# Feed-forward up projections as seven 2x2 block products (Strassen) instead of eight, on one Trainium2 core

## The reference, cut to what matters

```python
def _swiglu(h, w13, w2):            # w13: 1024 x 5632, w2: 2816 x 1024
    g, u = jnp.split(h @ w13, 2, axis=-1)
    return (jax.nn.silu(g) * u) @ w2

def _sublayer(x, fn, pre_g, post_g, shift, scale, gate, res_w):
    h = _rmsnorm(x, pre_g) * (1.0 + scale[:, None, :]) + shift[:, None, :]
    y = _rmsnorm(fn(h), post_g)
    return x + res_w * (1.0 + gate[:, None, :]) * y
```

## Time and profile before

| what | value |
|---|---|
| median of the runs | 3217.52 us |
| lowest to highest | 3217.0 to 3223.48 us |
| span of the profiled execution, first to last instruction | 3213.7 us |
| PE busy | 3045.3 us (95%) |
| PE weight loads busy | 2461.7 us (77%) |
| DVE busy | 1728.6 us (54%) |
| ACT busy | 1155.9 us (36%) |
| POOL busy | 1349.1 us (42%) |
| mean DMA rate | 114 GB/s |

### The profile page before, as it was taken

The page is one execution under the profiler, slowest core; times in us unless marked ns, Lnnn a source line. Parts: engine busy times, 40 slices in busy tenths (PEclk is TensorE's granted clock), DMA queues, the critical chain, the costliest instruction groups (busy, mean ns, idle before and its releaser), DMA issues. The chain is left out here.

```text
span 3213.7 us, 52487 instructions
## 1 busy us (share of the span) xinstructions
PE 3045.3 (95%) x20065; PEld 2461.7 (77%) x20065; DVE 1728.6 (54%) x3224; ACT 1155.9 (36%) x2075; POOL 1349.1 (42%) x893
## 2 busy tenths in 40 slices
PE   5999999899999999999999999999888889999998
PEld 4888876678887888877788887987666667778887
DVE  6445478654445566232666114537677754674443
ACT  3222235432223322234332223226544434435343
POOL 3444443244444434453434444224767660143332
PEclk8999999999999999999999999999999999999999
DMA  7655432155544554332255334213222233222222
GB/s 216 195 184 173 158 85 73 53 170 183 183 156 153 167 180 135 97 90 79 86 163 151 94 93 136 79 53 112 65 58 58 56 107 73 91 77 71 82 66 59
DMA packets 641381, 366.02 MB, mean 114 GB/s; under 512 B 107902, under 2 KB 634132, under 8 KB 640688
## 3 DMA queue, kind: packets, MB, share of 16 engines
q1 hardware_dynamic: 633216, 351.57, 37.2%
q10 hardware_dynamic: 6640, 10.49, 1.1%
q0 software_dynamic: 1344, 1.44, 0.2%
HBM read 334.27 MB, written 24.97 MB: 112 GB/s over the span
## 5 line engine op out<-in xcount | busy, mean ns | idle before, releaser
L270 POOL TENSOR_TENSOR w_lo<-w_raw,w_hi 128x1024 fp32r<-128x1024 f32 (+1 forms) x333 | 786.6, 2362 | 1316.6 <-ACT w_hi L262 1263.9
L335 PE MATMUL acc<-h,w_hi 128*128 128x512 f32 x2256 | 704.4, 393 | 0.0
L262 ACT ACTIVATE w_hi<-w_raw 128x1024 fp32r<-128x1024 f32 (+1 forms) x332 | 344.6, 1038 | 941.1 <-PE acc L335 687.9
L335 PEld LDWEIGHTS acc<-h,w_hi 128*128 128x128 f32 x2256 | 417.3, 188 | 84.6 <-issue 1.8
L335 PE MATMUL acc<-h,w_lo 128*128 128x512 f32 x1128 | 440.3, 390 | 0.0
L335 PE MATMUL acc<-hid,w_hi 128*128 128x512 f32 x1056 | 326.3, 390 | 0.0
L716 DVE SCALAR_TENSOR_TENSOR ada_part<-ada_raw,c_act,ada_part 128x256 f32<-128x256 f32 x672 | 315.0, 489 | 18.6
L335 PEld LDWEIGHTS acc<-h,w_lo 128*128 128x128 f32 x1128 | 211.7, 188 | 45.8
L335 PEld LDWEIGHTS acc<-hid,w_hi 128*128 128x128 f32 x1056 | 197.3, 188 | 40.7
L335 PE MATMUL spare<-h,w_hi 128*128 128x512 f32 x688 | 211.7, 389 | 0.0
L335 PE MATMUL acc<-hid,w_lo 128*128 128x512 f32 x528 | 205.6, 389 | 0.0
(11 more groups left out here) (700 smaller groups left out, 6094.7 us busy)
## 6 DMA issues: line engine op xcount, KB each, us to landing
w_raw<-in_ffn_w SPq DMA_DIRECT2D x240, 512.0 KB, 4.0
ada_raw<-in_ada_w SPq DMA_DIRECT2D x88, 1024.0 KB, 5.0
w_raw<-in_od_w_in SPq DMA_DIRECT2D x32, 512.0 KB, 4.0
w_raw<-in_ffn_w SPq DMA_DIRECT2D x32, 384.0 KB, 3.1
w_raw<-in_ev_w_in SPq DMA_DIRECT2D x22, 512.0 KB, 3.9
image<-inverse_wait SPq DMA_DIRECT2D x144, 64.0 KB, 2.1
first_ada<-in_ada_w SPq DMA_DIRECT2D x8, 1024.0 KB, 12.4
w_raw<-in_ab_w_in SPq DMA_DIRECT2D x16, 512.0 KB, 4.0
```

The source lines that it names most:

```text
L262: act.activation(K.w_hi[:, first % SPLIT, 0:tiles, :], K.raw[:, first % RAW, 0:tiles, :], ACT.Copy).then_inc(K.hi_ready, 1)
L270: pool.tensor_tensor(K.w_lo[:, first % SPLIT, 0:tiles, :], K.raw[:, first % RAW, 0:tiles, :], K.w_hi[:, first % SPLIT, 0:tiles, :].bitcast ...
L335: mm = pe.matmul(out, w[:, slot, k, :], moving(ap, k, tokens), start=first and k == 0 and p == 0, stop=last and k == tiles - 1 and p == le ...
```

## The change

The up products of turns 3 to 21 are made in another way (turns 0 to 2 stay, `PLAIN = 3`). Tokens are halved (`HALF` = 256) and so is the depth of the product (`KH` = 4 of 8 blocks). With g and u as the two rows, this is a 2x2 by 2x2 block product, and seven block products p = 1 to 7 replace eight. Each is 4 tiles x 3 passes = 12 products of 256 columns.

- The four sums of h blocks (`term`, 1024 elements each) are made once a sub-layer by DVE, with hi parts by ACT (`term_hi`) and lo parts by DVE (`term_lo`). For them h is needed in full: ACT writes every h block twice (L501, L503), and DVE's lo part is now `full - hi`, both in SBUF.
- The four sums of weights are made each turn by DVE (`sums_first`, `sums_second`: one op of 1024 elements, two of 512). ACT makes seven hi parts and POOL seven lo parts of 512 elements a turn, one turn ahead of TensorE, in two sets of slots.
- The products land in seven half banks of PSUM. ACT copies product 1 to SBUF; DVE combines them (`combine_left`, `combine_right`, `combine_outer`), ACT takes silu, DVE the gated product (`gated`). The next turn's product 1 waits for `left`, product 5 for `u_second`, product 3 for `outer`.
- The gated values are kept in full (`hid_full`) and split into hi and lo only after the last turn: hi by ACT (`hidden_hi`), lo by DVE for 17 of 22 and by POOL for values 8 to 12. The first down turn waits tile by tile.
- Modulation chunks: one vector of one chunk a turn, in three pieces (`ada_part`) between the combinations, by a table; sub-layer 0 has 19 in its up turns and 7 in its down turns, 2 has 19 and 8, 3 has 11 of one vector and 4 of two vectors (a vector a turn) and 8 of two in its down turns, 5 has 4 of two and 8 of two.
- Loops over turns are written out. The scratch of the DMA descriptors is made 8192 bytes.

```diff
-def quick_pre_act(act, K, S, base, shift, update=True, between=None):
+def quick_pre_act(act, K, S, base, shift, update=True, between=None, full=None):
...
         act.activation(S.h[:, HI, b, :], S.tp[b % 2][:], ACT.Identity, bias=shift[:, b:b + 1]).then_inc(S.h_hi, 1)
+        if full is not None:
+            act.activation(full[:, b, :], S.tp[b % 2][:], ACT.Identity, bias=shift[:, b:b + 1]).then_inc(S.h_full, 1)
...
     def low(b):
+        if full is not None:
+            dve.wait_ge(S.h_full, b + 1)
+            dve.tensor_tensor(S.h[:, LO, b, :], full[:, b, :], S.h[:, HI, b, :].bitcast(F32), ALU.subtract).then_inc(S.h_ready, 1)
+            return
...
+        def slots_free(eng, t):
+            if t >= PLAIN + 2:
+                eng.wait_ge(S.turn_done, t - PLAIN - 1)
...
+                for t in range(PLAIN + 2, FB):
+                    n = base + 2 * t
+                    sp.wait_ge(S.lo, 7 * (t - PLAIN - 1))
+                    chunk_load(n + 1, up.sources[1](t))
+                    sp.wait_ge(S.left_done, t - PLAIN - 1)
+                    chunk_load(n, up.sources[0](t))
+                    ada_until(t)
...
+                for t in turns:
+                    for p in (1, 5, 7, 2, 6, 3, 4):
+                        lo(t, p)
...
+                for j in range(8, 13):
+                    pool.wait_ge(S.hid_hi, j + 1)
+                    pool.tensor_tensor(hid[:, j, :], hid_full[:, j, :], hid_hi(j).bitcast(F32),
+                                       ALU.subtract).then_inc(S.hid_pool, 1)
...
+                def product(t, p):
+                    pe.wait_ge(S.lo, 7 * (t - PLAIN) + LO_PLACE[p])
+                    for k in range(KH):
+                        for part in (HI, LO):
+                            pe.matmul(out_of[p], hi_of(t, p)[:, k, :], moving[p][:, part, k, :], start=k == 0 and part == HI, stop=False)
+                    for k in range(KH):
+                        mm = pe.matmul(out_of[p], lo_of(t, p)[:, k, :], moving[p][:, HI, k, :], start=False, stop=k == KH - 1)
+                    if p in done:
+                        mm.then_inc(done[p], 1)
...
+                    if tau == 0:
+                        pe.wait_ge(S.prod_ready, 2)
+                        pe.wait_ge(S.h_full, DB)
+                        pe.wait_ge(S.t_ready, 4)
+                    else:
+                        pe.wait_ge(S.left, tau)
+                    product(t, 1)
+                    product(t, 2)
...
+                    product(t, 6)
+                    if tau:
+                        pe.wait_ge(S.u_second, tau)
+                    product(t, 5)
+                    product(t, 7)
+                    if tau:
+                        pe.wait_ge(S.outer, tau)
+                    product(t, 3)
+                    product(t, 4)
...
+                def sums_first(t):
+                    tau = t - PLAIN
+                    slots_free(dve, t)
+                    chunk_landed(dve, t, 0)
+                    chunk_landed(dve, t, 1)
...
+                    dve.tensor_tensor(both, quarters[:, 2:3].broadcast_to([P, 2, KH * P]), quarters[:, 0:4:3],
+                                      ALU.subtract).then_inc(S.sums, 1)
+                    dve.wait_ge(S.sums, 3 * tau + 1)
+                    dve.tensor_tensor(sum_full(t, 6), full_of(t, 1), sum_full(t, 5),
+                                      ALU.subtract).then_inc(S.sums, 1)
...
+                for t in turns:
...
+                    if t > PLAIN:
+                        combine_outer(t - 1)
+                    if t + 1 < FB:
+                        sums_first(t + 1)
+                    if t > PLAIN:
+                        gated(t - 1)
+                    ada_piece(0, 2)
+                    combine_left(t)
+                    if t + 1 < FB:
+                        sums_second(t + 1)
+                    ada_piece(2, 5)
+                    combine_right(t)
+                    if pending is not None:
+                        ada_write(dve, K, S, ada, pending)
+                    ada_piece(5, DB)
...
+                hidden_lo(0, 4)
+                combine_outer(FB - 1)
+                hidden_lo(4, 8)
+                gated(FB - 1)
+                hidden_lo(13, FB)
```

More of the change, by code:

```diff
@@ new lines, in ada_load, with ada_landed, ada_part @@
+def ada_load(sp, K, q):
+    source, i = K.ada_of(q)
+    if q >= ADA:
+        sp.wait_ge(K.ada_used, FIRST_ADA + q - 1)
+    sp.dma_start(K.ada_raw[:, q % ADA], source(i)).then_inc(K.ada_landed[q % ADA], 16)
+def ada_landed(dve, K, q):
+    dve.wait_ge(K.ada_landed[q % ADA], 16 * (q // ADA + 1))
+def ada_part(dve, K, S, steps, q, v, lo, hi):
+    source, i = K.ada_of(q)
+    final = v == source.vecs - 1
+    for k in range(lo, hi):
+        col = K.cact[:, source.use[v], k:k + 1]
+        out = K.ada_acc[:, v, :] if k == DB - 1 else S.ada_part[:, v, :]
+        if k == 0:
+            if v == 0:
+                ada_landed(dve, K, q)
+            ins = dve.tensor_scalar(out, K.ada_raw[:, q % ADA, k, :], col, None, ALU.mult)
+        else:
+            steps.all()
+            ins = dve.scalar_tensor_tensor(out, K.ada_raw[:, q % ADA, k, :], col, S.ada_part[:, v, :], ALU.mult, ALU.add)
+        if k == DB - 1 and final:
+            ins.then_inc(K.ada_used, 1)
+        else:
+            steps.start(ins)
@@ L909, in ffn_phase, with ada_write @@
+def ada_write(dve, K, S, steps, q):
+    source, i = K.ada_of(q)
+    ada_columns(dve, K, steps, FIRST_ADA + q, source.bias(i), source.out(i), source.vecs, S.ada_cols)
 def ffn_phase(K, index, layer, sub, which):
     nc, A = K.nc, K.A
-    seg = K.weights.phases[index]
-    up, down = seg[:-1], seg[-1]
-    u0 = up[0]
+    up, down = K.weights.phases[index]
+    base = up.base
     shift, scale, gate = (K.mod_cols(layer, sub, kind) for kind in range(3))
     tiles = (8, 8, FB - 16)
+    turns = range(PLAIN, FB)
+    count = len(turns)
@@ L950, in _ @@
+                for c in range(2, 3 * DB):
+                    split_lo(pool, K, down, c // 3, c // 3, c % 3, tiles[c % 3])
                 split_next(pool, K, index, split_lo)
@@ L1036, in _ @@
-                for n in range(4):
-                    block_turn(n, n)
-                loop(pe, 4, DB, 4, block_turn)
+                        multiply(pe, K, down, n, n, j, tiles[j], [(banks[n % 4][:], LAT)],
+                                 lambda p, k, sl, j=j: hid_hi(8 * j + k) if p == HI else hid[:, 8 * j + k, :],
+                                 first=j == 0, last=j == 2, before=(lambda k, j=j: operand_ready(8 * j + k)) if n == 0 else None)
+                    if n == 0 and pending is not None:
+                        ada_pe(pe, K, FIRST_ADA + pending, K.ada_of(pending)[0].vecs, K.ada_acc, S.ada_cols)
```

430 lines of the change are left out of this document (321 added, 109 removed).

## The result

The changed kernel takes 3347.4 us (median of 4 runs, 3343.2 to 3348.6) against 3217.3 before, measured beside it: 1.040 times as long, 95% interval 1.0384 to 1.0415. The forecast had 3262, with a range of 3170 to 3325. The sign was right, the size was not: +130 us, not +45. The profiled execution has a span of 3346.7 us, 133.0 more than before.

What follows compares the result with a forecast made beforehand. TensorE bounds the kernel before; in the new up turns DVE and POOL, excluding each other, would. -40 + 20 + 21 + 32 + 15 - 3 = +45 us on a span of 3213.7, plus 3.8 carried over: 3262 us, range 3170 to 3325.

Steps and rivals of the forecast that it cites:

- Chunks: Modulation chunks moved into down turns of sub-layers 3 and 5: +15 us; chunks of turns 1 and 2 moved: -3.
- seam: From the up turns to the first down block, hidden values now rounded after the turns: +8 four times, +32 us.
- Turns: Up turns 3 to 21: 11.1 us each, as DVE and POOL exclude each other; sum 837.8 against 878.2, -40 us.
- Rival 1: Up turns: TensorE stays the bound, turns at 10.5 us, 3175 us in all, faster; chance 0.22.
- rival 2: Up turns: DVE bounds, its four two-input ops each waiting a whole POOL op, 11.9 us a turn, 3322 us; chance 0.12.
- Start: First stage: h's second full copy lengthens DVE's and ACT's chain; +6.5 us in sub-layers 2, 3 and 5, +20.
- Entry: Before turn 3: DVE's sums and low parts make TensorE wait 5.3 us, four times, +21 us.
- Loads: Weight loads in the up turns: costed at nothing, or 1.5 us a turn if their cover is gone.
- rival 3: Up turns: loads come late, 1.5 us a turn, 3374 us; chance 0.03.
- rival 4: Up turns: 256-column products paced by their weight loads, 15.8 us a turn, 3620 us; chance 0.01.

Runs made afterwards that it cites:

- Run 2: Changed kernel, but in a down turn ACT squares and scales the last block before rounding the third weight chunk: 3277.6 us.
- run 1: Changed kernel, but TensorE sums the modulation chunk left over from the last up turn before the first down block: 3336.4 us.
- run 11: Changed kernel with the edits of run 1, Run 2, Run 3 and run 4, and TensorE's chunk sum moved behind the next down turn's first weight chunk: 3210.0 us.
- run 6: Changed kernel with DVE's first combination (one input in PSUM, one in SBUF) made twice in each turn: 3348.6 us, one execution.
- Run 3: Changed kernel, but DVE makes h's low part from the block in PSUM and ACT writes the full copy after that: 3333.5 us.
- Run 10: Kernel of run 9, with DVE pausing after the thirteenth hidden low part until POOL's low part of the third weight chunk is made: 3335.3 us.
- run 4: Changed kernel, but ACT writes silu into a free PSUM bank instead of SBUF, except in the last turn: 3316.7 us.
- run 8: Changed kernel with the edits of run 1, Run 2, Run 3 and run 4, and product 4's low weights made by DVE instead of POOL: 3277.3 us.
- run 9: Changed kernel, but DVE makes the low parts of all 22 hidden values and POOL none of the five: 3351.7 us.
- run 13: Kernel of run 11 with run 9's edit added and without Run 3's edit: 3214.7 us.

## Why the prediction was wrong

**The step that failed** is in "Chunks": "DVE's 8.3 us for one lies under a down turn of 15.0 us." The length was right, 7.3 us. What I left out is when it may begin. In a down turn DVE first has the block's border work, and that waits for ACT, which stands behind the rounding of the third weight chunk: 9 us of idle DVE, 3 of border, 7.3 of chunk. A one-vector chunk just fits (the down turns of sub-layers 0 and 2 are 15.6 us before and after), a two-vector chunk doesn't. Run 2 moves two ACT instructions and gives 70 us back. I compared a duration with a length and did not ask, as for the seam, what is queued ahead. The rows to see it stand in the trace of the kernel before, and I had read none. This is DVE in a down turn of sub-layer 0 there, which began at 353.92, with a one-vector chunk:

```profile
361.75 1.31 DVE L640 TENSOR_TENSOR scaled<-z,x 128x512 f32<-128x512 f32 x1 [7.50 <-ACT z L581]
...
364.84 0.48 DVE L714 TENSOR_SCALAR ada_part<-ada_raw,c_act 128x256 f32<-128x256 f32 x1
...
368.50 0.48 DVE L716 SCALAR_TENSOR_TENSOR ada_acc<-ada_raw,c_act,ada_part 128x256 f32<-128x256 f32 x1
```

The chunk ends 15.1 us into a turn of 15.6. A second vector's 3.2 us (7.3 for two against 4.1 for one) had no room, and the wait measured is 3.0.

**Behind the first block** the same sum is later still: TensorE idles 5.1, 5.1, 10.4 and 7.0 us in sub-layers 0, 2, 3 and 5. The edits of runs 1 and 11 together leave 1.7 us in sub-layers 3 and 5 and nothing in the others. The late sums, here and in the later down turns, account for the 96 us that "Chunks" lacked in the down stages: 62.8 of waits, 28.8 of slower products behind them, and 4 by which the sums themselves are over the 14.7 forecast.

**Turns: right in mechanism, a little short in size.** Forecast 11.1 us a turn by what DVE and POOL exclude, measured 11.25; the sum 837.8, measured 846.8 up to the last product. (In that sum sub-layer 5 has 11.0 for all eighteen turns, though seven of them hold a chunk; at 11.1 for those it would be 0.7 more.) PE is no longer full and POOL is busy 21.11 of 22.52 us, as written. Rival 1 (TensorE stays the bound) is out, and so is rival 2 as stated: DVE is busy 21.82 of the 22.52 but part of that is being held off, and run 6 gave it 0.6 us more for nothing.

**Start: right.** Forecast +20, measured +19.6 (24.23 us for the stage in sub-layer 2, "near 25"), 6.1 in each of sub-layers 2, 3 and 5 and 1.2 in sub-layer 0, where nothing was forecast. Run 3 bears out the chain through the second copy.

**Entry: too dear.** Forecast +21, together with -3 for the chunks of turns 1 and 2; measured +1.0 for both. TensorE idles 1.3 to 1.5 us before turn 3, not 5.3: one of the two weight sums of 512 elements and two of the h sums met POOL idle, 0.69 and 1.22 us instead of the 2.8 and 2.3 that I took. DVE in sub-layer 2:

```profile
686.78 2.77 DVE L1338 TENSOR_TENSOR z<-w_raw,z 128x512 f32<-128x512 f32 x1
689.59 0.69 DVE L1344 TENSOR_TENSOR rest_of_h<-w_raw,z 128x512 f32<-128x512 f32 x1
690.20 1.22 DVE L1314 TENSOR_TENSOR h_terms_full<-hid_full 128x1024 f32<-128x1024 f32 x1
```

I had priced each meeting near its dear end. With the shorter start of run 3 the idle time is 3.2 to 3.5, so some of what the entry saves here the start has paid.

**Seam: right in kind, somewhat dear.** Forecast +32, measured 24.9: 18.3 in the first blocks, which are 19.1 to 20.1 us and not 23, and 6.6 ahead of them. Run 10 shows the exclusion in half of it.

**Loads: costed at nothing, right.** ACT does wait for them, 53.4 and 42.4 us in the list of waits in all, but the turn is only 0.15 us over the forecast where rival 3 had 1.5, and run 4 shortens it with the same loads, so rival 3 is out. Turns of sub-layer 5 without a chunk in run 8 are 84 products in 10.1 us, 0.12 each, so rival 4 is too.

So of the 88 us that the span is over the forecast's sum, +96 come from the chunks in the down stages, +8 from the borders (half of it one more late sum) and +9 from the turns, less 17 at the entry and 7 at the seam. Entry and seam, 24 us too dear, hid part of what the forecast lacked; that is luck. The range's upper end, 3325, was built from rivals in the up turns, the stage that the change rewrites. The loss lay in the stage that only took over leftover work.

## What to carry to other kernels

Before moving work under a longer stage, find when its engine is free there: idle time in one block of a turn is worth the work's length only if nothing it needs stands behind a wait. Count DVE and POOL ops with both inputs in SBUF as one queue; an operand put into a free PSUM bank takes DVE out of it. See whether a sum that TensorE takes at the end of a turn can be taken one piece of work later; here that gave 25 us.

## What was not expected of the hardware

- DVE's two-input ops in SBUF, one behind the other without a gap, left POOL no room at all: its op of 1.85 us lasted 8.4 (run 9). When POOL too had ops queued, in the changed kernel's seam, DVE's four took 1.7 us each and POOL's five 1.6. A pause of DVE gave POOL its place (run 10).
- A DVE product of 8 elements took 2.36 us instead of 0.17 beside a POOL op of 2.40 (run 1): here the hold did not depend on how much DVE had to read.
- The same turns, in the same order, ran at 10.7 us in sub-layer 0 and 10.9 in sub-layer 2 of one run (runs 11 and 13). What sets the rhythm isn't shown.
- After 1.5 us of idle TensorE and eight products of one column, and after 3.0 us as well, the next products were slower by 1.6 us in all, at a lower granted clock.
